# One attention and one mixer kernel on TensorE: another order for the rotation, the output pieces and the last beats

## What is computed

```python
def rope(x, cos, sin):
    xf = x.astype(jnp.float32)
    x1, x2 = jnp.split(xf, 2, axis=-1)
    return jnp.concatenate([x1 * cos - x2 * sin, x2 * cos + x1 * sin], axis=-1).astype(x.dtype)

def swa_sink_attention(q, kk, vv, sinks):
    ...
    s = jnp.einsum('bnqhgd,bnkhd->bnhgqk', qb, kk)
    ...
    s = jnp.where(valid[None, :, None, None], s, NEG_INF)
    m = jnp.maximum(jnp.max(s, axis=-1, keepdims=True), sink)
    p = jnp.exp(s - m)
    denom = jnp.sum(p, axis=-1) + jnp.exp(sink - m)[..., 0]
    o = jnp.einsum('bnhgqk,bnkhd->bnhgqd', p, vv) / denom[..., None]
...
    m = swa_sink_attention(q, kk, vv, sinks[j]) @ w_o[j]
...
def mlstm(q, k, v, i_pre, f_pre):
    ...
    Dm = jnp.where(causal, b[..., :, None] - b[..., None, :] + ig[..., None, :], -jnp.inf)
    m = jnp.maximum(bq, jnp.max(Dm, axis=-1))
    Wt = jnp.exp(Dm - m[..., None]) * jnp.einsum('bhcld,bhcsd->bhcls', qc, kc)
...
    def compress(t, pe, w1, w2):
        flat = blk.reshape(B, G, Nc, CMP_BLOCK * dh)
        return jax.nn.gelu(flat @ w1.astype(f32)) @ w2.astype(f32)
...
        x = x + jnp.concatenate([m_out, a_out], axis=-1) @ w_out[i]
```

## Time and profile before

| what | value |
|---|---|
| median of 3 timed runs | 1629.02 us (1628.95 to 1630.65) |
| the profiled execution, its own time | 1630.3 us |
| its span on the core | 1628.6 us |
| TensorE, busy | 1591.5 us, 98% of the span |
| VectorE, busy | 1009.4 us, 62% |
| ScalarE, busy | 705.3 us, 43% |
| GpSimd, busy | 173.8 us, 11% |
| share of the chain that ended last | PE 93%, DVE 4% |
| mean granted TensorE clock | 0.991 of full speed |

### The profile page before, as it was taken

How to read it: one execution, slowest core, us unless ns; L and a number is a source line. 1 busy time by engine, 2 the same in 40 slices (tenths; PEclk the granted TensorE clock), 3 DMA queues, 4 the chain that set the end, 5 groups by cost and what they waited for, 6 DMA issues and landing times.

```text
span 1628.6 us, 21356 instructions
## 1 busy us (share of the span) xinstructions
PE 1591.5 (98%) x8046; PEld 1290.6 (79%) x8046; DVE 1009.4 (62%) x1886; ACT 705.3 (43%) x1383; POOL 173.8 (11%) x164
## 2 busy tenths in 40 slices
PE   8999999999998999999999999999999999999997
PEld 7888888888875788888888887766765888888887
DVE  5876666544866577766653376666666555554367
ACT  7544444333545545444432343344444443443252
POOL 0121111000012202111110000000001001110000
PEclk9999999999999999999999999999999999999998
DMA  5233333333220213333332433211110222223231
GB/s 205 73 110 96 97 98 98 106 107 110 77 83 1 71 57 94 97 96 92 98 103 97 139 104 106 65 46 46 40 40 27 97 91 98 97 98 97 97 110 66
DMA packets 91151, 143.69 MB, mean 88 GB/s; under 512 B 8740, under 2 KB 30756, under 8 KB 90920
## 3 DMA queue, kind: packets, MB, share of 16 engines
q1 hardware_dynamic: 88560, 136.58, 27.0%
q10 hardware_dynamic: 2488, 5.75, 1.1%
HBM read 140.19 MB, written 2.10 MB: 87 GB/s over the span
## 4 chain that ended last, share of the span: by engine, by line
PE 93%; DVE 4%; issue 1%; ACT 1%; POOL 0%; DMA 0%; SPq 0%; POOLq 0%; DVEq 0%; ACTq 0%
PE ps L447 23%; PE ps L449 23%; PE ps L448 23%; PE ps L1953 2%; PE ps L1955 2%; PE ps L1954 2%; PE ps L1634 1%; PE ps L1657 1%; PE ps L1677 1%; PE ps L488 1%; PE ps L490 1%; PE ps L489 1%; PE ps L1323 1%; DVE Hl L595 1%; PE ps L1352 1%
## 5 line engine op out<-in xcount | busy, mean ns | idle before, releaser
L432 DVE TENSOR_TENSOR wl<-raw,wh 128x512 fp32r<-128x512 f32 (+2 forms) x419 | 303.1, 727 | 403.4 <-ACT wh L423 402.9
L423 ACT ACTIVATE wh<-raw 128x512 fp32r<-128x512 f32 (+2 forms) x419 | 260.7, 626 | 541.3 <-PE ps L449 537.6
L447 PE MATMUL ps<-Hh,wh 128*128 128x512 f32 x1088 | 427.2, 393 | 0.9 <-DVE Hl L1428 0.9
L449 PE MATMUL ps<-Hh,wl 128*128 128x512 f32 x1088 | 424.0, 390 | 0.0
L448 PE MATMUL ps<-Hl,wh 128*128 128x512 f32 x1088 | 424.0, 390 | 0.0
L447 PEld LDWEIGHTS ps<-Hh,wh 128*128 128x128 f32 x1088 | 204.6, 188 | 45.0 <-issue 1.5
L448 PEld LDWEIGHTS ps<-Hl,wh 128*128 128x128 f32 x1088 | 204.6, 188 | 42.8 <-issue 0.5
L449 PEld LDWEIGHTS ps<-Hh,wl 128*128 128x128 f32 x1088 | 204.5, 188 | 42.9
L447 PE MATMUL ps<-AH,wh 128*128 128x512 f32 x416 | 161.8, 389 | 0.0
L448 PE MATMUL ps<-AL,wh 128*128 128x512 f32 x416 | 161.8, 389 | 0.0
L449 PE MATMUL ps<-AH,wl 128*128 128x512 f32 x416 | 161.8, 389 | 0.0
(11 more groups left out here) (335 smaller groups left out, 2281.7 us busy)
## 6 DMA issues: line engine op xcount, KB each, us to landing
raw<-in_w_in SPq DMA_DIRECT2D x216, 256.0 KB, 2.7
raw<-in_w_out SPq DMA_DIRECT2D x104, 256.0 KB, 2.6
raw<-in_w_up SPq DMA_DIRECT2D x64, 256.0 KB, 2.6
raw<-in_w_down SPq DMA_DIRECT2D x32, 256.0 KB, 2.6
raw<-in_w_q SPq DMA_DIRECT2D x16, 256.0 KB, 2.6
raw<-in_w_o SPq DMA_DIRECT2D x16, 256.0 KB, 2.6
raw<-in_w_pg SPq DMA_DIRECT2D x16, 256.0 KB, 2.6
X<-in_xT SPq DMA_DIRECT2D x8, 256.0 KB, 4.3
```

Of the source, the lines that this page charges most:

```text
L423: e.activation(split_in[n][0][:, 0:width], raws[n % NRAW][:, 0:width], ACT.Copy, scale=1.0 if gain is None else gain).then_inc(s_hi, 1)
L432: e.tensor_tensor(wl[:, 0:width], raw, wh[:, 0:width].bitcast(F32), ALU.subtract).then_inc(s_lo, 1)
L447: e.matmul(b, wh[:, o:o + w], xh, start=k == 0, stop=False, skip_group_check=joined)
L449: m = e.matmul(b, wl[:, o:o + w], xh, start=False, stop=k == (nk - 4 if closing else nk - 1), skip_group_check=joined)
```

## The change

Six edits.

1. `turned` is cut in two. `cosine` writes the copy times the cosine straight into the turned row (`wk` or `wq`), not back into `M`; `turned` adds the sine product there. The cosine products stand earlier: those of turns 1 and 2 before `q1` 0 and 1, those of turns 3 and 4, with both copies, before beat 6; turn 3's sums stand before beat 7, turn 4's after beat 8.
2. Beat 0 waits for 4 sine products; the wait for 6 stands before the first transposes, in beat 2.
3. `o0` pieces are issued in halves of two tiles (six products), one behind each of beats 7 to 15; behind beat 16 stand the second half of piece 4 and the first of 5, behind beat 17 the second of 5, behind beat 18 all of 6 and 7. Splits and closings stay with the first half.
4. `w1[0]` is loaded once the squares of `z0` are added, `w1[1]` at `z1` 0; they swap places. The compression waits for `w1[0]` first and for `w1[1]` and `w2` at its third step.
5. The decay's exponential stands in the next beat, behind that beat's exponentials and copies.
6. Fills 0 to 5 stand a beat earlier (31 to 36), the first three waiting only for the last piece but one, and `w0` 0 to 3 stand in beats 35 to 38 (before: 0 to 2 in beats 36 to 38).

```diff
-        def multiply(e, n, outs, xh, xl, k, nk, closing=False, joined=False, late=()):
+        def multiply(e, n, outs, xh, xl, k, nk, closing=False, joined=False, late=(), part=None):
...
-            o = 0
+            o = 2 * P if part == 1 else 0
...
-                elif i == len(outs) - 1:
+                elif i == len(outs) - 1 and part != 0:
...
-        WIN += [("tcopy", 1), ("tcopy", 2), ("q1", 0), ("turn", 1), ("turned", 1), ("q1", 1), ("turn", 2), ("turned", 2)]
+        WIN += [("tcopy", 1), ("tcopy", 2), ("cosine", 1), ("q1", 0), ("turn", 1), ("turned", 1), ("cosine", 2), ("q1", 1),
+                ("turn", 2), ("turned", 2)]
...
-        WIN += [("tcopy", 3), ("beat", 6), ("tcopy", 4), ("turn", 3), ("turn", 4), ("beat", 7), ("turned", 3), ("o0", 0),
-                ("beat", 8), ("o0", 1), ("beat", 9), ("turned", 4), ("beat", 10), ("beat", 11), ("o0", 2), ("beat", 12),
...
+        WIN += [("tcopy", 3), ("tcopy", 4), ("cosine", 3), ("cosine", 4), ("beat", 6), ("turn", 3), ("turn", 4),
+                ("turned", 3), ("beat", 7), ("o0", 0, 0), ("beat", 8), ("turned", 4), ("o0", 0, 1), ("beat", 9), ("o0", 1, 0),
+                ("beat", 10), ("o0", 1, 1)]
+        for i in range(5):
+            WIN += [("beat", 11 + i), ("o0", 2 + i // 2, i % 2)]
+        WIN += [("beat", 16), ("o0", 4, 1), ("o0", 5, 0), ("beat", 17), ("o0", 5, 1), ("beat", 18)]
+        WIN += [("o0", 6 + i // 2, i % 2) for i in range(4)]
...
+        def dve_cosine(e, t):
...
             for i in range(2):
-                q = M[:, m0 + i, :]
-                e.scalar_tensor_tensor(q, q, scale, T[3], ALU.mult, ALU.mult).then_inc(s_tu, 1)
+                e.wait_ge(s_tq, 2 * t + i + 1)
+                e.scalar_tensor_tensor(turn_out(t, i), M[:, m0 + i, :], scale, T[3], ALU.mult, ALU.mult).then_inc(s_tu, 1)
...
-                    e.wait_ge(s_ts, 6)
+                    e.wait_ge(s_ts, 4)
...
+            MIX += [("lstm_exp", *LSTM[b - 9])] * (b >= 9 and LSTM[b - 9][1] < 4)
...
-            elif b > 35:
-                MIX += [("w0", b - 36)]
+            elif b > 34:
+                MIX += [("w0", b - 35)]
...
-            if 32 <= b < 38:
-                MIX += [("fill", b - 32)]
+            if 31 <= b < 37:
+                MIX += [("fill", b - 31)]
...
-                e.wait_ge(s_w1, 32)
+                e.wait_ge(s_w1, 16)
                 e.wait_ge(s_zev, 10)
+            if k == 3:
+                e.wait_ge(s_w2, 32)
...
+                    if what == "z0" and k == 7:
+                        e.wait_ge(s_sum, 7 * 3 + 7)
+                        load_w1(e, 0, s_w1)
```

More of the change, by code:

```diff
@@ L156, in build @@
         assert o_ + 6272 <= 2 * FT * 2048, o_
-        w1 = [at(f"b_w1{i}", [P, 16, P], m_at + 8192 * i) for i in range(2)]
+        w1 = [at(f"b_w1{i}", [P, 16, P], m_at + 8192 * (1 - i)) for i in range(2)]
         Sb = [at(f"b_Sb{i}", [P, 2, S], m_at + 4096 * i) for i in range(4)]
@@ L1330, in pe_beat @@
                     e.wait_ge(s_wcp, u)
+                else:
+                    e.wait_ge(s_ts, 6)
                 for s in range(4):
@@ L1456, in pe_window @@
                     outs = [banks[WIN_BANK[what] + n][:, :] for n in range(4)]
-                    if what == "q0" and k < LATE:
+                    if what == "o0":
+                        multiply(e, WIN_PIECE[what] + k, outs[2 * i[1]:2 * i[1] + 2], Hh[:, k, :], Hl[:, k, :], k, 8,
+                                 part=i[1])
+                    elif what == "q0" and k < LATE:
                         multiply_late(e, WIN_PIECE[what] + k, outs, 1, k)
@@ L1464, in act_window @@
             for what, *i in WIN:
-                if what in WIN_PIECE:
+                if what in WIN_PIECE and i[1:] != [1]:
                     k = i[0]
@@ L1512, in dve_window @@
                     dve_turn(e, i[0])
+                elif what == "cosine":
+                    dve_cosine(e, i[0])
                 elif what == "turned":
@@ L1863, in act_lstm, with act_lstm_exp @@
                 e.activation(lane_col(h, 0), LB[:, 0:4], ACT.Abs).then_inc(s_mabs, 1)
+        def act_lstm_exp(e, h, s):
+            d = DECAY[s][:, s * P:S]
+            e.wait_ge(s_md, 4 * h + s + 1)
+            e.activation(d, d, ACT.Exp).then_inc(s_me, 1)
         def gpsimd_lstm(e, h, s):
@@ L2104, in dve_gates, with load_w1 @@
                 e.tensor_scalar(gsig[:, 0, 0:24:3], gsig[:, 0, 0:24:3], col("rv", 0), None, ALU.mult).then_inc(s_gst, 1)
+        def load_w1(e, n, s_in):
+            e.dma_start(w1[n][:, :, :], A["cmp_w1"][n].rearrange("(c p) m -> p c m", p=P)).then_inc(s_in, 16)
         def act_second(e):
@@ L2122, in act_second @@
                         e.dma_start(w2[:, :, :], A["cmp_w2"]).then_inc(s_w2, 16)
+                    if what == "z0" and k == 7:
+                        e.wait_ge(s_sum, 7 * 3 + 7)
+                        load_w1(e, 0, s_w1)
                     if what == "z1" and k == 0:
                         keep_root(e, PRE_CHAIN[3], J_BANKS[3][STAT_BANK])
-                        for n in range(2):
-                            e.dma_start(w1[n][:, :, :],
-                                        A["cmp_w1"][n].rearrange("(c p) m -> p c m", p=P)).then_inc(s_w1, 16)
+                        load_w1(e, 1, s_w2)
                 elif what == "cmp" and i[0] == 5:
@@ L2147, in act_second @@
                     e.activation(big[:, MO + h, :], big[:, MO + h, :], ACT.Tanh, scale=0.5).then_inc(s_mo, 1)
+                elif what == "lstm_exp":
+                    act_lstm_exp(e, *i)
                 elif what == "lstm":
@@ L2152, in act_second @@
                     k = W_ORDER[c]
-                    if c == 0:
-                        e.wait_ge(*used[first["wo2"] - 1])
+                    if c in (0, 3):
+                        e.wait_ge(*used[first["wo2"] - (2 if c == 0 else 1)])
                     if k < 4:
```

16 lines of the change are left out of this document (4 added, 12 removed).

## The result

| what | before | after |
|---|---|---|
| median (lowest to highest), 4 runs each | 1629.84 us (1628.95 to 1630.69) | 1621.45 us (1620.34 to 1622.05) |
| the profiled execution, its own time | 1630.3 us | 1622.05 us |
| its span | 1628.6 us | 1620.3 us |
| mean granted clock | 0.991 | 0.995 |

What follows compares the result with a forecast made beforehand. TensorE, busy 98% of the span, bounds the kernel; only its standstills and half-clock time can be won. Window 6.6, compression 0 and mixer 1.3 sum to 7.9 us off 1629.0: 1621.1 us, range 1616.8 to 1625.4.

Steps and rivals of the forecast that it cites:

- Beat 0, 0.8 gained: Window start: TensorE's 0.78 us wait for turn 2's sine product before the first scores goes; gain 0.8 us.
- Beat 8, 2.4 us of wait for 0.5: Window: the 2.41 us wait for turn 3's last row goes; up to 0.7 us on GpSimd's second select remains, 0.5 taken.
- the Trainium skill's rule: Two-SBUF-input VectorE instructions and SBUF-reading GpSimd instructions exclude each other; beat 8 would wait 0.3 us, output piece 0 1.6.
- Waits of beats 12 and 16 and of piece 6: Window: new waits of about 0.4 us at beat 12, 0.3 + 0.6 at beat 16; 0.9 stays before output piece 6.
- Half an output piece behind each beat: Window: half pieces hide each unit's round; waits of 7.9 us fall to 2.7, gain 5.2 us, bounds 1.7 and 7.0.
- Crossings, 0.9 lost: Window: five half pieces where two beats met cost 0.17 us each, 0.9 us lost; bounds 0.5 and 1.5.
- The window's clock, 1.5 gained: Half-clock stretch from 505 to 510 us vanishes with the one standstill over 2 us; gain 1.5 us, bounds 0 and 1.5.
- Compression weights, nothing: Key compression: earlier weights and two semaphores gain nothing, since VectorE's fourth eviction ends the 3.10 us wait.
- The exponential: Second mixer, near 1229 us: ScalarE's copy comes 1.1 us forward, so 1.1 of TensorE's 2.2 us wait stays.
- The slower rival: Exponential comes too late: TensorE loses 0.8 us or more in each of 16 beats, 1633.9 us; chance 0.04.
- Fills and piece 0, some 1.3 us lost against 1.1 gained: Last beats: piece 0 waits 1.3 us, closing root 1.0; the old 1.0 falls to 0.2, 0.7 to 0.5.

Runs made afterwards that it cites:

- the run with the take first: Changed kernel with VectorE's second four evictions of the mixer's projection moved ahead of the last two block copies: 1616.60 us, 0.9920 to the kernel before.

## Why the prediction was right, and where a term was not

The time was forecast at 1621.1 us and came out at 1621.45. Step by step:

- **Beat 0, 0.8 gained.** Right: TensorE's wait before the first scores is gone, and beat 2's transposes start at 472.38 instead of 473.02 us, 0.6 sooner, though TensorE came to beat 0 0.1 later.
- **Beat 8, 2.4 us of wait for 0.5.** Right: 0.37 us, on GpSimd's select as named. The size was between the row's 0.7 and the 0.3 that the Trainium skill's rule gave (page "SBUF — State Buffer", section "Who interferes with whom"). The trace agrees with the rule here: the select takes 0.97 us beside the cosine products in two kernels and 0.64 without them.
- **Waits of beats 12 and 16 and of piece 6.** Right: 0.38, 0.41 + 0.54 and 0.94 us against 0.4, 0.3 + 0.6 and 0.9.
- **"Half an output piece behind each beat": the waits' sum right, the credit not.** The prediction put the waits of beats 9 to 11 down to pairs of beats having "nothing to hide behind: that is most of the 7.9 us". The pairs need VectorE's late products to wait for so long, and either remedy is enough. TensorE's waits from 484 to 562 us, without the one on turn 3's rows before beat 8 (5.5 is the kernel before and the run with turn 4's products late):

| | pieces whole | pieces halved |
|---|---|---|
| turn 4's products late | 5.5 | 2.1 |
| turn 4's products early | 3.5 | 2.6, of which 0.37 is on the select in beat 8 |

The halves take away 3.4 us where the products are late (and add 1.4 before beat 8) and 0.9 where they are early, and the changed kernel has both. So the halves add only the 0.9; the 2.4 us before beat 8 and 2.0 more go with the early products alone. This is the step of the prediction that failed, though the sum didn't show it.

- **Crossings, 0.9 lost.** 1.3 lost, 0.25 us for each of the five further half pieces and not 0.17. This term was mis-sized, and with 0.9 of waits gained the halving nets 0.4 us lost, which the equal medians can't tell from nothing. The half pieces, to which the prediction gave most of the window's gain, are worth nothing measurable beside the early products, and the sum came out none the less: in that respect it was luck.
- **The window's clock, 1.5 gained.** Right in sign: PEclk is 1.00 from 500 to 525 us. The prediction took 1.5 from one stretch; with the next one (0.96 from 510 to 515 us) the profile before lost 1.7. In another execution with that wait it was 3.4 us, so a single execution doesn't fix it.
- **Compression weights, nothing.** Right: the wait stays 3.1 us, the weights put back change nothing, VectorE's order changes it. The clock behind it costs up to 3.4 us, for the 2.3 that the prediction read from one stretch, which is why the run with the take first gained more than the wait.
- **The exponential.** Right: the copy is waited for 1.0 us for 2.2 (1.1 expected), and the clock behind it loses 1.7 us less. The slower rival didn't come: the median of the experiment that puts it back is higher, and none of the 16 beats shows a wait of 0.8 us for it.
- **Fills and piece 0, some 1.3 us lost against 1.1 gained.** Right in sign. Piece 0 waits 0.88 us (1.3 forecast; the 1.6 by the Trainium skill's rule, same page and section, was further off: VectorE's subtraction, 0.68 us from 1228.47 us, is over before GpSimd's sum begins at 1229.74, so the two never met and this place doesn't test the rule), the closing root 0.78 (1.0). Undoing them takes 0.7 us of waits away. The mixer's waits thus gained 0.3 us where 0.2 lost was forecast.

The two profiles can be held against this sum by position. The first product of output piece 6 starts 552.56 - 545.99 = 6.6 us sooner, as forecast for the window; the compression 1005.46 - 998.87 = 6.6 us sooner, so nothing was gained between; and the span is 8.3 us shorter, which leaves 1.7 for the mixer, 0.4 over its forecast. The measured terms give 0.6 + 5.3 - 1.3 + 1.7 = 6.3 for the window and 0.3 + 1.7 = 2.0 for the mixer: each is right to 0.3 us, and the two differences cancel.

**Open.** Why the same standstill draws 1.7 us of clock in one execution and 3.4 in another was not settled; the profiles show only that it does. At the compression, with a wait of 3.0 to 3.2 us each time, six profiles lost 3.4 us and three lost 1.7. This also bears on single medians: one such difference is larger than what several of the edits are worth.

## What to carry to other kernels

When an engine in a chain of small steps waits in several beats in a row, look first for one long piece of work in front of the chain on another engine, here 1.8 us of products in VectorE's queue, and move it to where that engine idles. Finer pieces between the beats hid the same waits, but each cut cost 0.25 us. Where two edits can cure the same wait, price each with the other in place: their gains don't add. In this kernel a standstill of over 2 us on TensorE was worth its own length and up to 3.4 us of clock behind it, so halving it can be worth more than removing several short ones. And a sum that comes out doesn't prove its terms: change one part at a time.

## What was not expected of the hardware

- The clock's drop came in this case's profiles after or in standstills of 2.2, 2.41, 3.1 and 3.78 us, but it also came in one execution amid waits of 0.88 and 1.29 us, which drew none in two other kernels with the same waits. Behind the standstills of the window stage, the compression and the last beats the loss was 1.7 or 3.4 us each time, by stretches of 5 us. Between executions of the kernel with the exponential put back, mean clocks of 0.992 to 0.995 go with 1625.85 to 1621.99 us.
- The start of the program has such a drop too, longer or shorter by chance: from 30 to 40 us the mean clock was 0.75 and 0.57 in the kernel before, 1.00 and 0.66 in the changed one, though nothing there was changed. The clock gave the changed one 1.7 us there, but this wait, which the kernel before didn't have, took 0.95 of it back, others before it took more, and at 39.44 us the changed kernel was 0.3 us behind (39.11 before):

```profile
36.30 0.58 PE L488 MATMUL ps<-Hh,xh 128*128 128x256 f32 x1 [0.95 <-DVE Hl L595]
```
